# Two moves in a written-out order: a roping pulled ahead of the first heads' sums, and a turn of keys ahead of a rounding of weights

## The chip, the cores and the metric

The kernel runs on one core of a Trainium2 chip. The metric is device time in microseconds (us) from start to end of one execution, lower is better. The engines named here are TensorE (PE in the profile, with its weight loads as PEld), VectorE (DVE), ScalarE (ACT), GpSimd (POOL) and SyncE (SP), whose queue issues the loads of weights.

## The reference, cut to what matters

Two small networks of two layers each run one after the other on 256 tokens of width 1024. The second mixer of the first network is block attention ("moba"). With 256 tokens there is one block of 256 keys, so it is causal attention with 16 heads of 64:

```python
qkv = (h @ w_qkv).reshape(Bsz, S, 3, N_HEADS, HEAD_DIM)
...
q = rope(q, pos) * (HEAD_DIM ** -0.5)
k = rope(k, pos)
...
s_own = jnp.einsum('bhqd,bhjd->bhqj', qc, ko).astype(jnp.float32)
s_own = jnp.where(kpos[None, :] <= qpos[:, None], s_own, NEG_INF)
p = jax.nn.softmax(jnp.concatenate([s_sel, s_own], axis=-1), axis=-1).astype(v.dtype)
...
return o @ w_o
```

`rope` multiplies the two halves of each head by cosines and sines: `[x1*cos - x2*sin, x2*cos + x1*sin]`. All else (short convolution, feed-forward layers, state space mixer, two further attentions) is left as it is by the change.

## The kernel before, in words

Every weight matrix comes in chunks of 128 x 2048 numbers. A chunk is loaded by SyncE into one of 4 buffers, rounded by ScalarE to a high part (line 1273, one of 5 buffers), and the rest is made on VectorE as a low part (line 1623, one of 4 buffers). TensorE multiplies high by high, high by low and low by high (line 1022): a projection step `tK.T` takes the 128 rows of the contraction with number K for the 128 tokens of tile T and is three matmuls of 512 columns here. SyncE's load number i waits until both parts of chunk i-4 are made.

The order of all work is one list of steps, read by all engines. Each engine goes through the whole list and issues its own share of each step, in order, with waits on semaphores. For the block attention this list is written out by hand as a text, `MOBA`. Its stages are `q0 k0 v0 q1 k1 v1 moba_out`: queries, keys and values of heads 0 to 7, the same of heads 8 to 15, and the output projection. The words that matter here:

- `ropeH.Q.T`: VectorE ropes the queries (Q=1) or keys (Q=0) of half H, tile T, from an accumulator in PSUM to SBUF: four multiplies (lines 1815 to 1818), a wait for them, and two sums (lines 1820 and 1821). The four ropings of a half go through one counter, in the order of the list.
- `crossH.Q.I`: TensorE turns two pairs of heads of the roped queries or keys (line 1107, four transposes), which needs both tiles of that roping and the one bank that the turns and the turned probabilities share; ScalarE copies the result out (line 1363 for queries, 1368 for keys of the second half). The next turn needs that copy.
- `+h`: ScalarE rounds the next chunk (1273), after the last use of the buffer. `+l`: VectorE makes the next low part (1623).
- `sN`: TensorE's scores of heads N and N+1 (1063), VectorE's maxima (1787) and ScalarE's exponentials (1343, 1345). `nN`: VectorE normalises head N (1795 to 1798).
- `dN wN rN` (heads 0 to 7): VectorE turns squares of the probabilities (1806), GpSimd's queue writes them to DRAM (2153) and reads them back in the other order (2160). `uN` (heads 8 to 15): TensorE turns the probabilities itself (1073), ScalarE copies them.
- `p3`, `p7`: TensorE's sums of values for heads 0 to 3 and 4 to 7 (1097), ScalarE's rounding of them (1356), VectorE's low part (1737). `p7` needs the probabilities of heads 4 to 7 read back.

`t_bank_free` says what a stage's first step needs of the bank that it writes. For `v1` it is the roping of the second queries of the same tile:

```python
"v1": lambda: (s_rope, ROPE_AT["rope", 1, 1, t]),
```

In `k1` and `v1`, the numbered chunks used below are: 59 and 60 are the two chunks of `v1` itself; 61 to 64 are those of `moba_out`; chunk 61's low part is the first `+l` of `v1` and 62's the second; chunk 64's rounding is the `+h` beside `t4.0`.

Of the kernel before, what the change touches and what calls it, by code (L numbers as in the profile page):

```python
# [160 lines left out]
t7.1  # L161
@q1 t0.0 n1 d1 w0 t0.1 t1.0 +h w1 t1.1 t2.0 r0 +l +l vcopy0 t2.1 s2 n2 r1 d2 t3.0 t3.1 w2 t4.0 n3 d3 t4.1 t5.0 s4 w3 r2
t5.1 t6.0 t6.1 n4 d4 r3 +h +l +h t7.0 t7.1
@k1 t0.0 s6 w4 n5 d5 rope1.1.0 t0.1 t1.0 t1.1 w5 t2.0 t2.1 t3.0 t3.1 t4.0 n6 d6 t4.1 t5.0 p3 r4 r5 w6 t5.1 +h +l r6 t6.0 t6.1
t7.0 t7.1
@v1 t0.0 rope1.1.1 t0.1 cross1.1.0 t1.0 n7 d7 rope1.0.0 +h w7 t1.1 rope1.0.1 +l t2.0 r7 t2.1 cross1.1.1 t3.0 +l t3.1 +h t4.0 cross1.0.0
t4.1 s8 +l t5.0 cross1.0.1 n8 t5.1 p7 s10 t6.0 u8 vcopy1 t6.1 t7.0 n9 t7.1 n10
@moba_out s12 u9 t0.0 t0.1 n11 n12 +h t1.0 +l u10 t1.1 n13 u11 t2.0 p11 u12 s14 n14 n15 +l u13 t2.1 t3.0 +h p13 u14
t3.1 u15 e4 p15 e5 e6 e7 +l +h end
# [2155 lines left out]
```

## Time and profile before

| | us |
|---|---|
| median of 3 runs | 1201.04 (1200.89 to 1201.39) |
| the profiled execution, its own time | 1200.93 |
| span of the profiled execution | 1199.6 |
| TensorE busy (matmuls) | 1189.0 |
| VectorE, ScalarE, GpSimd busy | 885.4, 657.8, 63.1 |

The profile is of one execution. Busy time is the time in which an engine had an instruction in work; matmuls overlap one another, so a start of one often lies a little before the end of the last. Times in the trace count from the start of the span. A row of the timeline gives start, duration, engine, line, operation, output and input, the number of instructions merged, and in brackets the idle time before and what ended it.

### The profile page before, as it was taken

How to read it: one execution, taken by the hardware profiler on the slowest of the kernel's cores; microseconds unless marked ns; L12 is line 12 of the kernel's file. 1: busy time of each engine (PE TensorE's matmuls, PEld its weight loads, DVE VectorE, ACT ScalarE, POOL GpSimd, SP SyncE). 2: the span in 40 equal slices, each digit the busy share in tenths (PEclk: the TensorE clock that was granted, in tenths of full speed). 3: DMA queues.
4: the chain of work that ended last, by engine and by line, in shares of the span. 5: the costliest groups of instructions: out<-in, count | busy, mean ns of one | idle time of the engine just before them, and what ended most of it. 6: DMA issues, size and time to landing. Idle time of an engine off the chain costs nothing.

```text
span 1199.6 us, 16810 instructions
## 1 busy us (share of the span) xinstructions
PE 1189.0 (99%) x6733; PEld 1024.5 (85%) x6733; DVE 885.4 (74%) x1238; ACT 657.8 (55%) x863; POOL 63.1 (5%) x91
## 2 busy tenths in 40 slices
PE   9999999999999999999999999999999999999997
PEld 8888888888777888888898888888889978888886
DVE  6977989846886798883688877776467667777744
ACT  6545666634556666663588645444337775544430
POOL 0000000000120000000005200000012001000000
PEclk9999999999999999999999999999999999999999
DMA  9755455564654555556434556555526542755530
GB/s 355 253 207 193 170 182 191 186 224 160 228 181 157 189 178 176 207 191 216 163 109 142 188 207 237 193 193 194 178 91 229 176 141 106 252 204 176 195 122 35
DMA packets 33821, 221.09 MB, mean 184 GB/s; under 512 B 4032, under 2 KB 4432, under 8 KB 9168
## 3 DMA queue, kind: packets, MB, share of 16 engines
q1 hardware_dynamic: 30848, 210.52, 50.1%
q0 software_dynamic: 2752, 9.44, 2.3%
q8 instruction: 53, 0.87, 0.3%
q14 instruction: 24, 0.20, 0.0%
q10 hardware_dynamic: 144, 0.07, 0.0%
HBM read 217.37 MB, written 2.62 MB: 183 GB/s over the span
## 4 chain that ended last, share of the span: by engine, by line
PE 98%; DVE 1%; DMA 1%; ACT 0%; issue 0%; SPq 0%; ACTq 0%
PE ps L1022 42%; PE ps L944 24%; PE ps L950 15%; PE ps L952 4%; PE ps L966 2%; PE ps L963 2%; PE ps L962 2%; PE ps L1063 1%; PE ps L1097 1%; PE ps L1036 1%; PE ps L1073 1%; DMA t<-in_wts 1%; PE ps L1162 0%; PE ps L1146 0%; PE ps L977 0%; PE ps L1044 0%
## 5 line engine op out<-in xcount | busy, mean ns | idle before, releaser
L1022 PE MATMUL ps<-t,t 128*128 128x512 f32 (+4 forms) x2346 | 536.0, 385 | 1.4 <-DVE t L1821 1.4
L1623 DVE TENSOR_TENSOR t<-t,t 128x2048 fp32r<-128x2048 f32 (+3 forms) x200 | 448.9, 2257 | 101.2 <-PE ps L1022 87.7
L1022 PEld LDWEIGHTS ps<-t,t 128*128 128x128 f32 x2346 | 424.8, 188 | 84.4 <-issue 2.8
L1273 ACT CAST t<-t 128x2048 fp32r<-128x2048 f32 (+3 forms) x200 | 374.5, 1882 | 203.6 <-PE ps L1022 104.0
L944 PE MATMUL ps<-t,t 128*128 128x512 f32 x1274 | 305.8, 390 | 0.0
L944 PEld LDWEIGHTS ps<-t,t 128*128 128x128 f32 x1274 | 238.9, 188 | 51.2
L950 PEld LDWEIGHTS ps<-t,t 128*128 128x128 f32 x1456 | 187.2, 191 | 7.4
L950 PE MATMUL ps<-t,t 128*128 128x256 f32 x1456 | 189.5, 283 | 0.0
L1772 DVE TENSOR_REDUCE t<-ps 128x512 f32<-128x1024 f32 x40 | 49.0, 1225 | 44.3 <-PE ps L952 44.3
L1725 DVE SCALAR_TENSOR_TENSOR t<-t,t,t 128x254 f32<-128x254 f32 (+1 forms) x176 | 73.2, 479 | 10.2 <-ACT t L1298 10.2
L1338 ACT CAST t<-t 128x512 fp32r<-128x512 f32 x44 | 27.3, 619 | 91.2 <-DVE t L1756 91.2
L2124 POOL TENSOR_TENSOR t<-t,t 128x1 f32<-128x1 f32 x22 | 15.0, 681 | 868.0 <-DVE t L1678 455.4
L1737 DVE TENSOR_TENSOR t<-t,t 128x512 fp32r<-128x512 f32 x48 | 33.2, 693 | 35.0 <-ACT t L1338 32.2
L952 PE MATMUL ps<-t,t 128*128 128x512 f32 x182 | 58.0, 397 | 0.0
L962 PE MATMUL ps<-t,t 128*128 128x256 f32 x192 | 49.0, 288 | 0.0
L963 PE MATMUL ps<-t,t 128*128 128x256 f32 x192 | 48.0, 283 | 0.0
L1334 ACT ACTIVATE t<-t 128x512 f32<-128x512 f32 x42 | 26.4, 628 | 29.2 <-DVE t L1725 29.2
L1298 ACT ACTIVATE t<-t,t 128x256 f32<-128x256 f32 x88 | 39.7, 500 | 1.6 <-DVE t L2066 1.6
L963 PEld LDWEIGHTS ps<-t,t 128*128 128x128 f32 x192 | 36.7, 191 | 0.5 <-issue 0.2
L962 PEld LDWEIGHTS ps<-t,t 128*128 128x128 f32 x192 | 36.7, 191 | 0.5 <-issue 0.2
L1557 ACT CAST t<-ps 128x512 fp32r<-128x512 f32 x28 | 15.6, 588 | 34.9 <-PE ps L1036 34.8
L966 PE MATMUL ps<-t,t 128*128 128x256 f32 x192 | 30.9, 283 | 0.0
(228 smaller groups left out, 846.0 us busy)
## 6 DMA issues: line engine op xcount, KB each, us to landing
t<-in_wts SPq DMA_DIRECT2D x192, 1024.0 KB, 5.0
t<-in_rows POOLq DMA_DIRECT2D x12, 512.0 KB, 4.3
t<-in_wts SPq DMA_DIRECT2D x4, 528.0 KB, 3.8
spilled_probs<-t POOLq DMA_DIRECT2D x8, 192.0 KB, 4.1
t<-spilled_probs POOLq DMA_DIRECT2D x8, 192.0 KB, 4.1
t<-in_wts SPq DMA_DIRECT2D x2, 768.0 KB, 4.6
t<-in_wts SPq DMA_DIRECT2D x2, 592.0 KB, 3.8
t<-in_x_in SPq DMA_DIRECT2D x2, 512.0 KB, 4.4
```

Of the source, the lines that this page charges most:

```text
L944: mm(ps[:, bank + m, :], H[:, kt, cols[m]], XT[:, kt, :, :].rearrange("p c s -> p (c s)"), start=kt == order[0], stop=False)
L950: mm(ps[:, bank + m, 0:S], L[:, kt, cols[m]], XTh[:, kt, :], start=False, stop=False)
L952: ins = mm(ps[:, bank + m, :], H[:, last, cols[m]], XT[:, last, :, :].rearrange("p c s -> p (c s)"), start=False, stop=True)
L962: mm(o, H[:, kt, c], XTh[:, kt, :], start=kt == 0, stop=False)
L963: mm(o, L[:, kt, c], XTh[:, kt, :], start=False, stop=False)
L966: ins = mm(o, H[:, kt, c], XTl[:, kt, :], start=False, stop=kt == 7)
L1022: ins = mm(ps[:, bank, at:at + c1 - c0], a, w[:, k, c0:c1], start=first and part == 0, stop=kt == KTS[stage] - 1 and part == 2)
L1273: copy(wh[:, k, 0:w], wraw[:, r, 0:w]).then_inc(s_hi, 1)
L1298: activation(dst[:, sl], src[:, sl], ACT.Copy, scale=vcol(name, col + blk)).then_inc(done, 1)
L1623: tt(wl[:, k, 0:w], wraw[:, r, 0:w], wh[:, h, 0:w].bitcast(F32), ALU.subtract).then_inc(s_lo, 1)
L1725: ins = stt(out=o, in0=src[:, blk * S:(blk + 1) * S - n], scalar=vcol(name, col + blk + (taps - 1 - n) * stride), in1=o, op0=ALU.mult, op1 ...
L1772: nc.vector.reduce_sum(dst.rearrange("p (a s) -> p a s", a=2), halves, AX_X).then_inc(s_wide, 1)
```

## The change

Two words move in the list. `rope1.1.1`, VectorE's roping of the second queries of tile 1, moves from `v1` (behind `t0.0`) to `k1` (behind `d6`), so that on VectorE it stands ahead of the low part of the sums of heads 0 to 3 (`p3`) and of chunk 60's low part (`+l`). `cross1.0.0`, the first turn of the second keys, moves from behind `+h t4.0` to ahead of it, so that on TensorE it stands ahead of `t4.0` and on ScalarE ahead of the rounding of chunk 64.

```diff
-@k1 t0.0 s6 w4 n5 d5 rope1.1.0 t0.1 t1.0 t1.1 w5 t2.0 t2.1 t3.0 t3.1 t4.0 n6 d6 t4.1 t5.0 p3 r4 r5 w6 t5.1 +h +l r6 t6.0 t6.1
+@k1 t0.0 s6 w4 n5 d5 rope1.1.0 t0.1 t1.0 t1.1 w5 t2.0 t2.1 t3.0 t3.1 t4.0 n6 d6 rope1.1.1 t4.1 t5.0 p3 r4 r5 w6 t5.1 +h +l r6 t6.0 t6.1
 t7.0 t7.1
-@v1 t0.0 rope1.1.1 t0.1 cross1.1.0 t1.0 n7 d7 rope1.0.0 +h w7 t1.1 rope1.0.1 +l t2.0 r7 t2.1 cross1.1.1 t3.0 +l t3.1 +h t4.0 cross1.0.0
+@v1 t0.0 t0.1 cross1.1.0 t1.0 n7 d7 rope1.0.0 +h w7 t1.1 rope1.0.1 +l t2.0 r7 t2.1 cross1.1.1 t3.0 +l t3.1 cross1.0.0 +h t4.0
 t4.1 s8 +l t5.0 cross1.0.1 n8 t5.1 p7 s10 t6.0 u8 vcopy1 t6.1 t7.0 n9 t7.1 n10
```

No instruction is added or removed. The order of the four ropings and of the four turns among themselves stays.

## Rows read from the trace of the kernel before

**Rows 1.** Page, busy time of the engines
```profile
PE 1189.0 (99%) x6733; PEld 1024.5 (85%) x6733; DVE 885.4 (74%) x1238; ACT 657.8 (55%) x863; POOL 63.1 (5%) x91
```

**Rows 2.** Waits of TensorE, whole span: waiter, releaser, total, times, longest
```profile
PE ps L1022 <- DVE t L1821: 1.4, 1, 1.4
PE ps L1063 <- ACT t L1368: 0.8, 1, 0.8
```

**Rows 3.** Chain that ended last, 341 to 366 us: start, us, what
```profile
359.59 0.69 PE ps L1022 x3
...
361.74 0.86 PE ps L1063 x8
```

**Rows 4.** Timeline of TensorE, k1 and v1
```profile
342.89 4.42 PE L1022 MATMUL ps<-t,t 128*128 128x512 f32 x18
348.69 0.96 PE L1022 MATMUL ps<-t,t 128*128 128x512 f32 x3 [1.39 <-DVE t L1821]
...
355.57 0.95 PE L1022 MATMUL ps<-t,t 128*128 128x512 f32 x3
357.33 0.93 PE L1063 MATMUL ps<-t,t 64*128 64x128 f32 x8 [0.81 <-ACT t L1368]
...
360.21 1.53 PE L1097 MATMUL ps<-t,t 128*64 128x128 f32 x24
```

**Rows 5.** Timeline of VectorE, k1 and v1
```profile
343.62 0.69 DVE L1737 TENSOR_TENSOR t<-ps,t 128x512 fp32r<-128x512 f32 x1 [2.73 <-ACT t L1356]
...
346.43 0.42 DVE L1815 TENSOR_TENSOR t<-ps,t 128x256 f32<-128x256 f32 x1
...
348.22 0.42 DVE L1821 TENSOR_TENSOR t<-t,t 128x256 f32<-128x256 f32 x1
348.55 0.16 DVE L1795 RECIPROCAL t<-t 128x2 f32<-128x2 f32 x1
...
353.91 0.42 DVE L1821 TENSOR_TENSOR t<-t,t 128x256 f32<-128x256 f32 x1
354.25 4.49 DVE L1623 TENSOR_TENSOR t<-t,t 128x2048 fp32r<-128x2048 f32 x2
...
362.36 0.35 DVE L1798 TENSOR_SCALAR t<-t,t 128x256 f32<-128x256 f32 x1
...
366.79 0.29 DVE L1787 CUSTOM_DVE_ANT_0 t<-ps,t 128x128 f32<-128x128 f32 x1 [1.06 <-PE ps L1063]
```

**Rows 6.** Timeline of ScalarE, v1
```profile
353.34 0.59 ACT L1363 COPY t<-ps 128x512 f32<-128x512 f32 x1 [0.81 <-PE ps L1107]
354.79 1.91 ACT L1273 CAST t<-t 128x2048 fp32r<-128x2048 f32 x1 [0.86 <-PE ps L1022]
356.60 0.58 ACT L1368 COPY t<-ps 128x512 f32<-128x512 f32 x1
```

**Rows 7.** Timeline of TensorE's weight loads, v1
```profile
354.99 0.59 PEld L1107 LDWEIGHTS ps<-t,t 128*128 128x128 f32 x4
...
363.10 0.48 PEld L1073 LDWEIGHTS ps<-t,t 128*128 128x128 f32 x3
```

**Rows 8.** Timeline of GpSimd, read of head 6, write and read of head 7
```profile
348.23 0.75 POOL L2160 DMA_DIRECT2D t<-spilled_probs  x1 [2.63 <-DMA spilled_probs<-t]
350.28 0.56 POOL L2153 DMA_DIRECT2D spilled_probs<-t  x1 [1.30 <-DVE t L1806]
354.09 0.75 POOL L2160 DMA_DIRECT2D t<-spilled_probs  x1 [3.25 <-DMA spilled_probs<-t]
```

**Rows 9.** Timeline of SyncE's queue, load of chunk 65
```profile
356.60 0.33 SPq L2240 DMA_DIRECT2D t<-in_wts  x1
```

**Rows 10.** DMA issues: head 7's read; head 3's write; all reads (last number us to landing)
```profile
t<-spilled_probs POOLq DMA_DIRECT2D x1, 192.0 KB, 2.9
...
spilled_probs<-t POOLq DMA_DIRECT2D x1, 192.0 KB, 6.8
...
DMA to landing us min/median/max: 2.9/4.1/7.1
```

## The prediction

> **What bounds the kernel now.** I read the page first: TensorE is busy 1189.0 of a span of 1199.6 us [rows 1]. So only two things can move the time: one of the few places where TensorE stands still, or a new one. The next view is the list of what TensorE waited for over the whole span. It is very short, and two of its entries are the places that the diff touches [rows 2]: 1.4 us before a projection matmul, ended by the last sum of a roping (line 1821), and 0.8 us before scores (line 1063), ended by ScalarE's copy of a turn of keys (line 1368). Third I read the timelines of the engines from 340 to 367 us, to name the steps. The 18 matmuls from 342.89 are t5.1 to t7.1 of k1 and t0.0 of v1; what starts at 348.69 is t0.1 of v1; what starts at 357.33 is s8 [rows 4].
>
> **Why TensorE stands still at t0.1.** It writes the bank of the second queries of tile 1, so it needs rope1.1.1. VectorE has that roping behind the low part of p3 and chunk 60's low part. It stands idle for 2.73 us until 343.62, waiting for ScalarE's rounding of p3, then does both, and starts rope1.1.1 at 346.43. The roping ends at 348.22 + 0.42 = 348.64, and t0.1 starts 0.05 us later [rows 4, 5].
>
> **Why it stands still at s8.** The scores need the copy of cross1.0.0. ScalarE finished the copy of cross1.1.1 at 353.93, stood idle 0.86 us until t3.1 freed a buffer, rounded chunk 64 from 354.79, and only then copied, from 356.60 to 357.18 [rows 6]. The scores start 0.15 us later [rows 4].
>
> **First edit: what the roping costs and frees.** In its place it holds VectorE from 346.43 to the start of the next instruction at 348.55, which is 2.12 us; to its own end it is 2.21 us [rows 5]. Its new place is the idle stretch before 343.62, which began at 343.62 - 2.73 = 340.89, with d6. Its queries have been in PSUM since the end of q1, and rope1.1.0 is done. So it would run from 340.9 to 343.1, and the low part of p3 can start at 343.62 as before, with 0.5 us to spare. That idle stretch is the cover, and the move costs nothing. Were the cover gone, it would cost at most what it costs now, and t0.1 would wait as before. t0.1 then needs nothing late, and follows t0.0.
>
> The gain at this place is more than the 1.39 us of idle, since a stream that starts anew must fill again. The last matmul before the gap ends at 342.89 + 4.42 = 347.31, the three of t0.1 at 348.69 + 0.96 = 349.65 [rows 4]; in a running stream three take 0.69 us end to end [rows 3]. 349.65 - 347.31 - 0.69 = **1.65 us**. The bounds are 1.39 (idle alone) and 1.65; I take 1.65, as both ends of it are rows.
>
> VectorE's queue behind the old place (n7, d7, rope1.0.0, rope1.0.1, the low parts of chunks 61 and 62, the maxima of s8) starts 2.12 us earlier. I checked the one step in it that could meet TensorE: rope1.0.0 needs the end of k1, which is one projection step before 347.31, so 346.6; it would start after n7 and d7 at about 347.8. So the whole queue keeps its 2.12 us.
>
> **Second edit.** On TensorE cross1.0.0 comes three matmuls earlier, on ScalarE one rounding earlier. TensorE is 1.65 us early there. In the trace the weights of cross1.0.0 load from 354.99 [rows 7]; three matmuls and 1.65 us earlier that is 354.99 - 0.69 - 1.65 = 352.65. It needs two things. The roping rope1.0.1 ended at 353.91 + 0.42 = 354.33 [rows 5], and 2.12 earlier is 352.21. The copy of cross1.1.1 ended at 353.93 [rows 6], and 1.65 earlier is 352.28. Both are there with 0.37 us left, against 0.05 us that a release took above. The copy of cross1.0.0 then runs on ScalarE from about 353.5 to 354.1. TensorE reaches s8 at 355.57 + 0.95 = 356.52 less 1.65, so 354.87: the copy is 0.8 us early. Gain at s8: the scores end at 357.33 + 0.93 = 358.26; from the end of t4.1 at 356.52 they need 0.86 in a running stream [rows 3, 4]: 358.26 - 356.52 - 0.86 = **0.88 us**. The bounds are 0.81 (idle) and 0.88. Without the first edit the turn's weights would want to load at 354.30 with the roping ending at 354.33, so the second edit doesn't hang on the first.
>
> The rounding of chunk 64 moves behind the copy, to about 354.1, still 0.7 us earlier than the 354.79 of now. VectorE wants it only behind v1's last matmuls. It costs nothing.
>
> **What is late next.** From s8 on TensorE is 1.65 + 0.88 = 2.53 us early and VectorE only 2.12, so VectorE's lead shrinks by 0.41 us. The maxima of s8 and n8 feed the turn of head 8's probabilities (u8), whose weights load from 363.10, while n8 ends at 362.36 + 0.35 = 362.71 [rows 5, 7]. With 0.05 for the release 0.34 us are free and 0.41 are wanted: a new stall of **0.07 us**. Its bounds are 0 and 0.41. Past s12 VectorE has waited 1.06 us for TensorE [rows 5], so there it has room again, and the two lock together.
>
> The other late one is p7, which needs head 7's probabilities back from DRAM. GpSimd's queue has read 6, write 7, read 7. The write went out at 350.28, 1.30 us after the read of head 6, because it waited for d7. With d7 2.12 early it follows that read at once, at 348.23 + 0.75 = 348.98. Write and wait for it took 354.09 - 350.28 = 3.81 us, so the read goes out at about 352.8 and lands 2.9 us later at 355.7 [rows 8, 10]. p7 began at 360.21 [rows 4] and would begin at 357.68. There are 2.0 us left, where 3.2 were.
>
> But traffic moves too. SyncE's load of chunk 65 hangs on the low part of chunk 61, which ends 2.12 us earlier, so it goes out at 356.60 - 2.12 = 354.5 [rows 9], 1.7 us behind the read, where it was 2.5 behind. Reads of the same size took between 2.9 and 7.1 us in this trace [rows 10]. At 7.1 the read would land at 359.9 and p7 wait 2.2 us. I take 0, since a load starts to move bytes only after the read in front of it has moved most of its own. Here a rule speaks against the change: the Trainium skill, DMA: Bandwidth & Descriptors, section Queues, rings and completion order, says that each DMA engine goes round between the queues that have work, a packet at a time, so a small read gets no right of way over a 1 MB load. The spread of 2.9 to 7.1 us fits it; by that rule a read caught by the load would take the long figure, and the sum below would fall from 2.46 to 0.3 us.
>
> **The sum.** 1.65 + 0.88 - 0.07 = 2.46 us. Everything behind the block attention hangs on TensorE and moves with it. Span 1199.6 becomes 1197.1, the profiled execution's 1200.93 becomes 1198.5; it lies 0.11 under the median of 1201.04, which becomes **1198.6**. What this measurement can tell from no change is about 0.2%, 2.4 us, so a time of 1198.64. The forecast lies right on that line.
>
> **Rivals.**
>
> *VectorE becomes the pace-setter* (0.10). If the 0.34 us at u8 is not really free, all that counts is VectorE's own 2.12 us. Speaks for it: from 343.62 to 365.7 it has no idle time. Against: n8's end and the load of u8 are rows. Time 1201.04 - 2.12 = 1198.9.
>
> *p7 waits for part of the round trip, or cross1.0.0 for its copy* (0.14). A read between its 2.9 and 7.1 us, or a write that the nearer load holds up, eats 0.5 to 2.2 us; the 0.37 us at cross1.0.0 could also be missed. Time 1199.1 to 1200.8, middle 1200.0. Against: in the run before this read was the fastest of the eight.
>
> *The change does nothing* (0.07). If t0.1 waits at the same time for something else that ends then, or p3's low part slips, the wait stays. Against: the release is 0.05 us after the roping's end, and the same chunk served t0.0. Time 1201.0.
>
> *Slower* (0.05). The write of head 7 now goes out at 348.98, into the load of chunk 64, and its read near the load of chunk 65. The longest write read here took 6.8 and the longest read 7.1 us [rows 10]: 348.98 + 6.8 + 7.1 = 362.9 against p7's 360.21 of before, 2.7 us later, 1203.7. It decides as soon as the round trip is over 360.21 - 348.98 = 11.2 us; it was 6.7. It would need both extremes at once.
>
> *More than forecast* (0.04): the stall at u8 is not there and a restart costs more than the ends show, 2.6 to 2.9 us, 1198.3.
>
> The forecast itself has 0.60, with a range of 1198.2 to 1199.1.
>
> **How the numbers follow.** Half of the forecast's 0.60 lies under the 1198.64 line, somewhat more as the value is under it by a hair: 0.38; with the last rival that is 0.42 for faster. The other part of the forecast, the pace-setter, the partial waits and no effect make 0.53. Slower has 0.05. The range goes from 1198.1, under the last rival's time, up to 1200.5, which takes in most of the partial waits and leaves out no effect, slower and a rest: about 0.15.
>
> **What the profile after would show.** TensorE's list of waits without both entries, or with one of about 0.1 us at line 1073; a roping that starts at 340.9 right behind a turn of squares on VectorE; the low part of p3 at 343.6 as before; line 1107's third turn of v1 right behind six matmuls, and ScalarE's copy at line 1368 ahead of the rounding; s8 near 354.9 and p7 near 357.7. Wrong would be a wait of line 1097 for a DMA, a wait of line 1107 for line 1363 or 1821, or a wait of line 1022 still at v1's start.

## The result, and the profile after

The median of the changed kernel is 1203.95 us (1200.94 to 1206.28, 20 executions), that of the kernel before 1201.19 us (1200.77 to 1204.86, 20). The ratio is 1.0018, with a 95% interval of 1.001 to 1.0025. It is slower by 0.18% (0.23% by the two medians), beyond the interval but about the 0.2% that I had called no change, and far from the 1198.6 forecast. The profiled execution took 1204.28 us with a span of 1203.0, 3.4 more than before.

What TensorE waited for over the whole span, the first four entries (waiter, releaser, total, times, longest):

```profile
PE ps L1097 <- DMA t<-spilled_probs: 4.4, 1, 4.4
PE ps L1243 <- DVE t L1997: 1.2, 1, 1.2
PE ps L977 <- DMA t<-in_wts: 0.5, 1, 0.5
PE ps L1206 <- ACT t L1503: 0.2, 1, 0.2
```

Both entries of [rows 2] are gone. A new one of 4.4 us stands in their place: the sums of heads 4 to 7 (p7) wait for the read of probabilities from DRAM. The timeline of TensorE, k1 and v1, against [rows 4]:

```profile
343.10 5.11 PE L1022 MATMUL ps<-t,t 128*128 128x512 f32 x21
348.04 0.60 PE L1107 MATMUL ps<-t,t 128*128 128x128 f32 x4
...
354.99 0.93 PE L1063 MATMUL ps<-t,t 64*128 64x128 f32 x8
...
356.99 0.95 PE L1022 MATMUL ps<-t,t 128*128 128x512 f32 x3
362.33 2.82 PE L1097 MATMUL ps<-t,t 128*64 128x128 f32 x24 [4.39 <-DMA t<-spilled_probs]
```

The 18 matmuls of before run on into t0.1 as 21 without a gap, and s8 starts without one. This execution is 0.21 us later than the other at the start of this stretch (343.10 against 342.89). t5.1, the last projection step ahead of p7, ends at 357.94; before it ended at 360.28 (from the chain: 359.59 + 0.69 [rows 3]). So TensorE was 2.34 + 0.21 = 2.55 us ahead. Then it stood still to 362.33, and p7 took 2.82 us instead of 1.53.

VectorE, ScalarE and their order, against [rows 5] and [rows 6]:

```profile
341.03 0.39 DVE L1815 TENSOR_TENSOR t<-ps,t 128x256 f32<-128x256 f32 x1
...
342.79 0.42 DVE L1821 TENSOR_TENSOR t<-t,t 128x256 f32<-128x256 f32 x1
343.83 0.69 DVE L1737 TENSOR_TENSOR t<-ps,t 128x512 fp32r<-128x512 f32 x1 [0.63 <-ACT t L1356]
...
352.33 4.49 DVE L1623 TENSOR_TENSOR t<-t,t 128x2048 fp32r<-128x2048 f32 x2
```

```profile
353.70 0.59 ACT L1368 COPY t<-ps 128x512 f32<-128x512 f32 x1 [1.24 <-PE ps L1107]
354.22 1.91 ACT L1273 CAST t<-t 128x2048 fp32r<-128x2048 f32 x1
```

The roping fills VectorE's idle stretch and leaves 0.63 us of it; the copy of keys runs ahead of the rounding. All that is as forecast. The GpSimd queue and one row of SyncE's queue, against [rows 8] and [rows 9]:

```profile
348.93 0.75 POOL L2160 DMA_DIRECT2D t<-spilled_probs  x1 [3.12 <-DMA spilled_probs<-t]
349.67 0.56 POOL L2153 DMA_DIRECT2D spilled_probs<-t  x1
355.55 0.75 POOL L2160 DMA_DIRECT2D t<-spilled_probs  x1 [5.32 <-DMA spilled_probs<-t]
```

```profile
354.69 0.33 SPq L2240 DMA_DIRECT2D t<-in_wts  x1
```

The write of head 7 goes out right behind the read of head 6, as forecast (at 349.67 and not at 348.98, since that read itself went out later), but landed 5.6 us later, where it had taken 3.5. So its read went out at 355.55, later than before, and now 0.9 us behind the load of chunk 65, which had gone out 2.5 us behind it. It took 6.7 us instead of 2.9. DMA issues of that write and that read (last number: us to landing), against [rows 10]:

```profile
spilled_probs<-t POOLq DMA_DIRECT2D x1, 192.0 KB, 5.6
...
t<-spilled_probs POOLq DMA_DIRECT2D x1, 192.0 KB, 6.7
```

Four stretches of the same trace (stretch, its length, busy times with instructions of PE, PEld, DVE, ACT and POOL, then PEclk, the granted TensorE clock as a share of 2.4 GHz, and last the busy share and the GB/s of the DMA engines):

```profile
360.00:361.00 1.00, 0.00 (x0) 0.00 (x0) 0.76 (x4) 0.00 (x0) 0.00 (x0) 1.00 0.86 347
361.00:362.00 1.00, 0.00 (x0) 0.00 (x0) 0.00 (x0) 0.00 (x0) 0.00 (x0) 0.80 1.03 401
362.00:363.00 1.00, 0.67 (x7) 0.70 (x9) 0.00 (x0) 0.00 (x0) 0.00 (x0) 0.50 0.90 336
...
365.00:366.00 1.00, 1.00 (x11) 0.59 (x9) 0.20 (x1) 0.59 (x1) 0.00 (x0) 1.00 0.16 66
```

While TensorE stood idle its clock fell to 1.2 GHz, and p7 ran wholly at that level. It is back in the stretch from 365.00, while p7 ends at 365.15. The Trainium skill, TensorE: Matmul & The Clock Gate, section Part 1: The HAM clock gate, says that an idle array falls to half its clock; the trace agrees. The loss adds up: the scores behind p7 end at 366.00, where they ended at 362.60 before, 3.40 us later, and the spans differ by the same 3.4.

### The profile page after: what moved, and what is told of

The parts are those of the page before. It is cut to its first block, busy times and chain, and to the rows that moved or that the text cites. A ratio compares the mean times of both kernels' runs of the same rounds, so it can differ in the third digit from the quotient of the medians.

```text
span 1203.0 us, 16810 instructions
## 1 busy us (share of the span) xinstructions
PE 1190.3 (99%) x6733; PEld 1026.0 (85%) x6733; DVE 885.6 (74%) x1238; ACT 658.9 (55%) x863; POOL 63.5 (5%) x91
## 4 chain that ended last, share of the span: by engine, by line
PE 97%; DMA 2%; DVE 0%; POOL 0%; issue 0%; ACT 0%; SPq 0%; POOLq 0%
PE ps L1022 42%; PE ps L944 24%; PE ps L950 14%; PE ps L952 4%; PE ps L966 2%; PE ps L963 2%; PE ps L962 2%; PE ps L1063 1%; PE ps L1097 1%; PE ps L1036 1%; PE ps L1073 1%; DMA spilled_probs<-t 1%; DMA t<-spilled_probs 1%; DMA t<-in_wts 1%; PE ps L1162 0%; PE ps L1146 0%
```

## The experiments

My theory after the result: head 7's round trip through DRAM is late, since its write runs into the load of chunk 64 and its read into the load of chunk 65, both of which the earlier roping brought together. The rivals: the moved turn does harm by itself; the round trip is long whatever the loads do; the earlier order of GpSimd's queue (write beside the read of head 6) is the cause. Edits are against the kernel before for e1, e2, e7 and e10, and against the changed kernel for the others, unless said.

**e1_rope_only.** The first edit alone.

```diff
-... n6 d6 t4.1 t5.0 p3 ...      @v1 t0.0 rope1.1.1 t0.1 ...
+... n6 d6 rope1.1.1 t4.1 t5.0 p3 ...      @v1 t0.0 t0.1 ...
```

> Only the roping is moved, the turn of keys stays where it was. Theory (read-back): TensorE gains 1.65 us at t0.1, the 0.8 us wait of the scores s8 stays, and the sums p7 then wait for head 7's read, whose write now goes out right behind the read of head 6, into the load of chunk 64, and which itself meets the load of chunk 65. Since the landing of the read sets the start of p7, the time is that of the full change, about 1203.9 (1202 to 1205), with a wait of 3 to 4 us at line 1097. Rival (the turn is what hurts, since it delays ScalarE's rounding of chunk 64): this kernel is faster than before, about 1199.5, with no wait at line 1097.

Measured: 1201.21 us (1200.56 to 1205.94), ratio 1.0007 (0.9998 to 1.0015). The profile shows the wait of p7, but of 1.0 us only, with a write of 5.3 and a read of 5.0 us, and a wait of 1.3 us at s8. The time is under the range that I expected. Of the 1.65 us of gain p7's wait took 1.0 and the longer wait at s8 (1.3 instead of 0.8) another 0.5, so p7 waits for the round trip as the theory has it, but for far less than I expected. The longer wait at s8 has a cause that I had not seen. ScalarE's rounding of chunk 64 waited for the load itself:

```profile
353.89 1.91 ACT L1273 CAST t<-t 128x2048 fp32r<-128x2048 f32 x1 [1.41 <-DMA t<-in_wts]
355.69 0.58 ACT L1368 COPY t<-ps 128x512 f32<-128x512 f32 x1
```

The load of chunk 64 took 7.0 us instead of 5.6. That the moved write did this isn't shown: in e2, with the write at its old place, the load took 7.2. With the turn ahead of the rounding, as in the full change, TensorE doesn't wait for this load.

**e2_turn_only.** The second edit alone.

```diff
-... t3.0 +l t3.1 +h t4.0 cross1.0.0
+... t3.0 +l t3.1 cross1.0.0 +h t4.0
```

> Only the turn of keys is moved. Theory (read-back): VectorE's queue and so head 7's write, its read and the load of chunk 65 keep their times; TensorE gains the 0.88 us at s8 and p7 still starts after the landing: about 1200.3, no wait at line 1097. Rival (the turn hurts): slower than before, 1202 or more.

Measured: 1200.98 us (1200.49 to 1201.1), ratio 0.9997 (0.9989 to 1.0006). The rival falls: the turn does no harm, and the read took 2.8 us. But I missed the gain, too. The wait for the copy is gone and a new one stands three steps on:

```profile
362.41 0.35 DVE L1798 TENSOR_SCALAR t<-t,t 128x256 f32<-128x256 f32 x1
...
362.91 0.52 PE L1073 MATMUL ps<-t,t 128*128 128x128 f32 x3 [0.27 <-DVE t L1798]
```

u8 starts at 362.91 instead of 363.33, 0.42 us earlier and not 0.88 (0.07 of it was there before, at t0.1): VectorE, not moved here, sets the pace from n8 on. The median moved by 0.11 us only; the rest of the 0.35 isn't accounted for. The prediction had the 0.34 us of room there; I didn't carry it into this expectation.

**e3_loads_later.** The full change with later low parts of chunks 61 to 63.

```diff
-... rope1.0.1 +l t2.0 r7 t2.1 cross1.1.1 t3.0 +l t3.1 cross1.0.0 +h t4.0 t4.1 s8 +l t5.0 cross1.0.1 n8 t5.1 p7 ...
+... rope1.0.1 t2.0 r7 t2.1 cross1.1.1 t3.0 t3.1 cross1.0.0 +h t4.0 t4.1 s8 t5.0 +l cross1.0.1 n8 t5.1 +l p7 ...
-... n11 n12 +h t1.0 +l u10
+... n11 n12 +h +l t1.0 +l u10
```

> The full change, and beside it VectorE's low parts of chunks 61 and 62 behind the maxima of s8 and that of chunk 63 behind n12, so that the loads of chunks 65 to 67 go out some 4 us and more later. The load of chunk 64, and with it the neighbourhood of head 7's write, stays. Theory (the read is held up by the load of chunk 65): the read lands in about 3 us instead of 6.7, p7 waits about 1 us or less and the clock of TensorE stays up: about 1199.5 (1198.6 to 1200.5). Rival (the round trip is long by itself, or by the load of chunk 64 alone): p7 waits 3 us or more, time as with the change, 1203 to 1204.

Measured: 1199.74 us (1199.6 to 1200.98), ratio 0.9987 (0.9978 to 0.9996), 4.2 us under the full change. The last write and the last read of its GpSimd queue, and the landing of that read:

```profile
349.90 0.56 POOL L2153 DMA_DIRECT2D spilled_probs<-t  x1
357.24 0.75 POOL L2160 DMA_DIRECT2D t<-spilled_probs  x1 [6.78 <-DMA spilled_probs<-t]
```

```profile
t<-spilled_probs POOLq DMA_DIRECT2D x1, 192.0 KB, 2.9
```

The load of chunk 65 went out at 359.66 and the read took 2.9 us. The write took 7.1 us beside the load of chunk 64, so p7 still waited 2.1 us in this execution, which is the slowest of its eleven. That is half of the theory: the read, met by no load, is short again.

**e4_write_early.** The full change, with head 7 normalised, turned and written ahead of the moved roping, and read right behind head 6.

```diff
-@k1 ... n6 d6 rope1.1.1 t4.1 t5.0 p3 r4 r5 w6 t5.1 +h +l r6 t6.0 t6.1
+@k1 ... n6 d6 w6 n7 d7 w7 rope1.1.1 t4.1 t5.0 p3 r4 r5 t5.1 +h +l r6 r7 t6.0 t6.1
-@v1 t0.0 t0.1 cross1.1.0 t1.0 n7 d7 rope1.0.0 +h w7 t1.1 rope1.0.1 +l t2.0 r7 t2.1 ...
+@v1 t0.0 t0.1 cross1.1.0 t1.0 rope1.0.0 +h t1.1 rope1.0.1 +l t2.0 t2.1 ...
```

> The full change, and beside it n7 and d7 right behind d6 on VectorE, ahead of the moved roping, the writes of heads 6 and 7 ahead of the reads of heads 4 and 5 and the read of head 7 right behind that of head 6 on the GpSimd queue. VectorE gets some 0.8 us more work ahead of the low part of p3 than its idle stretch holds, all of it work that it then has no more behind. Theory (read-back): the read lands by 353, p7 waits for nothing, and the 2.5 us that TensorE gains at t0.1 and s8 are all seen: 1198.6 (1198.2 to 1199.2). Rival (something else in the change costs time, as the turn or the clock): 1200 or more.

Measured: 1198.55 us (1198.38 to 1198.84), ratio 0.9979 (0.997 to 0.9987): faster than both kernels. Its start of p7 and its writes and reads:

```profile
356.92 0.95 PE L1022 MATMUL ps<-t,t 128*128 128x512 f32 x3
357.80 1.53 PE L1097 MATMUL ps<-t,t 128*64 128x128 f32 x24
```

```profile
341.32 0.54 POOL L2153 DMA_DIRECT2D spilled_probs<-t  x1 [2.88 <-DVE t L1806]
342.64 0.54 POOL L2153 DMA_DIRECT2D spilled_probs<-t  x1 [0.78 <-DVE t L1806]
343.68 2.99 POOL L2160 DMA_DIRECT2D t<-spilled_probs  x4 [0.49 <-PE ps L1097]
```

Both writes go out while no load is in flight and take 2.1 us each. Neither entry of [rows 2] nor one at line 1097 is in its list of waits. The gain of 2.5 us that the prediction worked out is all seen once the round trip is out of the way.

**e5_sums_later.** The full change, with p7 behind s10 and t6.0.

```diff
-... t5.1 p7 s10 t6.0 u8 vcopy1 t6.1
+... t5.1 s10 t6.0 p7 u8 vcopy1 t6.1
```

> The full change, and beside it the sums p7 two places later in the list (behind s10 and t6.0 instead of ahead of them), about 1.8 us of TensorE's work. Writes, reads and loads stay. Theory (read-back): the read lands as late as with the change, but the work put ahead of p7 fills 1.8 us of its wait, and where the wait that is left is short the clock does not fall: 1200.3 to 1202.2, about 1201.5. Rival (it is not the landing that sets p7 but the length of the list): no change against the full change, 1203.9.

Measured: median 1199.5 us (1199.2 to 1205.01), ratio 0.9994 (0.9985 to 1.0004). The rival falls, and the gain is more than I expected: in the profiled execution, the fastest of its eleven, write and read took 5.1 and 5.3 us, the wait was 0.4 us, and the clock stayed up. Some executions still reach 1205.

**e6_write_first.** The full change, with head 7's write ahead of head 6's read on the GpSimd queue.

```diff
-... t5.1 +h +l r6 t6.0 t6.1      ... rope1.0.0 +h w7 t1.1 ...
+... t5.1 +h +l t6.0 t6.1      ... rope1.0.0 +h w7 r6 t1.1 ...
```

> The full change, and beside it the write of head 7 ahead of the read of head 6 on the GpSimd queue, so that it goes out at about 348.2 instead of 349.7 and the read of head 6 goes behind it. The load of chunk 64 is in flight as before. Theory A (the write is slow because the read of head 6 runs beside it): the write lands in 4 us or less, by 352.3, and the read of head 7 goes out ahead of the load of chunk 65 at 354.7 and lands by 356: about 1198.8. Theory B (the write is slow because of the load of chunk 64): the write still takes 5 to 6 us, lands at 353.5 to 354, and the read then meets the load of chunk 65: 1200 to 1203.

Measured: 1202.62 us (1198.37 to 1206.17), ratio 1.0012 (1.0 to 1.0024). The write went out at 348.10, ahead of the read, and took 6.5 us beside the load of chunk 64 (out at 346.54). The time that theory A gave did not come. The run doesn't take the read of head 6 away, though: it went out at 348.75 and ran beside the write all the same, so e8 has to decide between A and B. Two of the twelve executions took 1198.37 and 1198.57 us, which is the full gain. The wait at p7 in the profiled one, and the clock:

```profile
360.12 2.83 PE L1097 MATMUL ps<-t,t 128*64 128x128 f32 x24 [2.45 <-DMA t<-spilled_probs]
```

```profile
361.00:362.00 1.00, 1.00 (x13) 1.00 (x12) 0.00 (x0) 0.00 (x0) 0.00 (x0) 0.50 1.03 418
```

**e7_before_early_write.** The kernel before with the early write of e4 and nothing else.

> The kernel before, with only n7 and d7 early on VectorE and the writes of heads 6 and 7 and the read of head 7 early on the GpSimd queue; the roping and the turn stay where they were before. Theory: the wait for the roping at t0.1 is left as it is, as the low part of p3 and of chunk 60 start at the same time; VectorE's queue behind the roping is 1.35 us earlier; the wait at s8 stays: 1200.5 to 1201.1. The read is then never the last to come, so the executions should lie within about 0.5 us of each other, where those of the kernel before reach up to 1204.9. If the outliers stay, they are of another cause than the read.

Measured: 1201.14 us (1200.84 to 1201.68), ratio 1.0 (0.9991 to 1.0009). That is a hair above the range that I expected: the early write is worth nothing by itself. Its executions lie within 0.84 us, but those of the kernel before beside it reached only 1202.5, so whether the read makes the rare executions of 1204 us of the kernel before stays open.

**e8_load64_later.** As e3, with the low part of chunk 60 behind rope1.0.0.

```diff
-... w6 t5.1 +h +l r6 t6.0 t6.1      ... n7 d7 rope1.0.0 +h w7 t1.1 ...
+... w6 t5.1 +h r6 t6.0 t6.1      ... n7 d7 rope1.0.0 +l +h w7 t1.1 ...
```

> As the kernel with the later loads (loads of chunks 65 to 67 later), and beside it VectorE's low part of chunk 60 behind rope1.0.0, so that the load of chunk 64 goes out at about 351.3 instead of 346.8, behind the write of head 7. Theory B (the write is slow because of the load of chunk 64): the write takes 3 to 3.5 us and lands by 353.2; the read of head 7 then goes out at 353.5 and meets the load of chunk 64 instead, taking 3 to 6 us. Theory A (the read of head 6 beside it is enough): the write takes 5 us or more. The time is a mix, as rope1.0.1 now ends at 353.4 and cross1.0.0 waits for it about 0.7 us: 1199.3 to 1202.

Measured: 1200.26 us (1200.08 to 1200.85), ratio 0.9992 (0.9984 to 1.0001). The write and the read of head 7 on the GpSimd queue, and the landing of the write:

```profile
349.38 0.56 POOL L2153 DMA_DIRECT2D spilled_probs<-t  x1
352.53 0.75 POOL L2160 DMA_DIRECT2D t<-spilled_probs  x1 [2.59 <-DMA spilled_probs<-t]
```

```profile
spilled_probs<-t POOLq DMA_DIRECT2D x1, 192.0 KB, 2.9
```

The read of head 6 went out beside it as before (at 348.65), but the load of chunk 64 only 1.7 us behind it (at 351.07), and the write took 2.9 us. Theory A falls here. That is the other half, from one profiled execution: it is a load of chunk 64 already in flight that holds the write up. p7 waited for nothing. The rest of the gain went to waits on VectorE's and ScalarE's later work (0.3 at a turn, 0.5 at s12, 0.7 at u9).

**e9_early_write_rope and e10_early_write_turn.** e4 with one of the two edits each (e4 with `+h t4.0 cross1.0.0` as before; e7 with `cross1.0.0 +h t4.0`).

> The kernel with the early write of head 7, with the roping moved and the turn of keys left where it was before. With the read-back off the path, the roping's own term should stand by itself: 1.65 us under the median of before, 1199.4, and the wait at s8 of about 0.8 us is back in the list of TensorE's waits. Rival (the terms are not additive, s8's wait follows the load of chunk 64): up to 1200.

> The kernel with the early write of head 7, with the turn of keys moved and the roping left where it was before. VectorE's queue behind the roping is 1.35 us earlier here than in the kernel with the turn alone, so the stall at u8 that took most of the 0.88 us there should be gone: 0.88 us under the median of before, 1200.2, and no wait at line 1073. Rival (the turn is worth only 0.1 to 0.3 us by itself): 1200.8 to 1201.0.

Measured: e9 1199.8 us (1199.53 to 1202.25), ratio 0.9985 (0.9976 to 0.9994); e10 1200.27 us (1199.87 to 1200.97), ratio 0.999 (0.9981 to 0.9999). e10 is 0.76 us under the 1201.03 of the kernel before beside it, near its 0.88, and has no wait at line 1073, which fits the room at u8 as what took the gain away in e2. e9 gains 1.23 instead of 1.65, as its rival had it. Its profiled execution shows how: s8 waits 1.7 us, since ScalarE's rounding in front of the copy waits 1.8 us for the load of chunk 64. But that execution is the slowest of its eleven (1202.25 us), so the size of the wait in the others isn't known. With both edits the copy is ahead of that rounding, and the sum is 2.5.

The landings side by side, each from one profiled execution (out, and us to landing):

```
              load 64        head 7's write   load 65   head 7's read   p7 waited
before        346.59  5.6    350.28  3.5      356.60    354.09  2.9     0
after         346.80  7.4    349.67  5.6      354.69    355.55  6.7     4.4
rope only     346.84  7.0    349.61  5.3      354.72    355.22  5.0     1.0
turn only     346.52  7.2    350.34  4.5      356.66    355.08  2.8     0
loads later   347.04  9.1    349.90  7.1      359.66    357.24  2.9     2.1
sums later    346.52  6.8    349.16  5.1      354.41    354.58  5.3     0.4
write first   346.54  7.5    348.10  6.5      354.43    354.85  5.1     2.4
load 64 later 351.07  5.1    349.38  2.9      359.65    352.53  4.2     0
write early   347.32  6.4    342.64  2.1      353.89    345.92  3.1     0
before, early 346.74  5.9    342.65  2.1      355.65    345.92  4.9     0
early, rope   347.31  6.8    342.63  2.1      353.88    345.89  3.3     0
early, turn   346.56  7.3    342.47  2.1      355.48    345.74  5.6     0
```

The last four rows are e4, e7, e9 and e10. Start and duration added give the landings, and these say more than the durations. With the read of head 6 ahead of it and the load of chunk 64 in flight, the write of head 7 landed 1.6 us behind that load before, and 0.8 to 1.1 us behind it in the five others (after, rope only, turn only, loads later, sums later). When the write itself went out, between 349.2 and 350.3, made next to no difference: with the rope only it went out 0.7 us earlier than with the turn only, and landed 0.1 us later. And the load's own duration, 5.6 to 9.1 us, doesn't follow the moved write: it was 7.2 with the write at its old place (turn only) and 7.3 with the write long landed and a read beside it (early, turn). Why it varies isn't shown. Of the reads with no load in flight ahead of them, those that a load followed by 0.8 us took 4.9 and 5.6 us, those that one followed by 1.4 us or more 2.8 to 3.3.

## Why the prediction was wrong

**Right, by its steps.** The cause of both waits, the cover of the roping (0.5 us to spare forecast, 0.63 seen), the 1.65 + 0.88 = 2.53 us on TensorE's side (2.55 seen at t5.1), the turn with its two needs met, and the copy at 353.70 against "about 353.5". The stall of 0.07 us at u8 never came to the test in the full change, as p7's wait hid it; e2 shows that the room of 0.34 us is real.

**The step that failed** is the one on p7: "Write and wait for it took 354.09 - 350.28 = 3.81 us, so the read goes out at about 352.8", and then "I take 0". I moved the write 1.3 us nearer to the load of chunk 64 and kept the duration of its old place. Behind that load it took 5.1 to 7.1 us in the five profiled executions where it went out at 348.1 to 349.9 (five rows of the table), and 2.9 ahead of it (e8). Its landing followed that of the load: the write went out 0.6 us earlier than before and landed 1.5 us later, at 355.26, as the load itself landed at 354.20 instead of 352.21. So the earlier roping brought the read nothing, while it did bring the load of chunk 65 forward by 1.9 us. The second half follows from the first. "I take 0" held for the order that it assumed: in e2, with the load 1.6 us behind the read, the read took 2.8 us. But by the forecast the read was 1.7 us ahead of the load of chunk 65; by the late write it came 0.9 us behind it, and took 6.7 instead of 2.9 us (2.9 again in e3). The rule of the Trainium skill that I had set beside it (DMA: Bandwidth & Descriptors, section Queues, rings and completion order: engines take turns between queues by packets) was against me here: a read caught by the load got no right of way. The traces agree in the durations, 5.0 to 6.7 us for the four reads that went out 0.2 to 0.9 us behind the load; none of them was read down to the turns of the queues.

**The rival that came true** is the slower one, with a chance of 0.05. Its mechanism and place were right and its chance was far too small, for two reasons. I said that it needed both extremes at once (6.8 + 7.1), but its own threshold of 11.2 us was already passed by 12.5 (349.67 to 362.20). And I took the two transfers as independent, where a late write is what puts the read behind the load. Its price lacked a term as well: the clock at 1.2 GHz made p7 last 2.82 us instead of the 1.53 that it took at full clock behind the wait of e3, 1.3 us more. So it is partly luck that its 1203.7 lies next to the measured 1203.95: it had p7 at 362.9, later than the 362.33 seen, and nothing for the clock.

**What stays open.** The full change takes 2.7 us more in the median than the roping alone, where I expected the same. In the profiled executions p7 starts 2.0 us later and the clock costs 1.3. Why its read should be the longer one in most executions, when both order the same transfers at nearly the same times, isn't shown. The traces give two hints. In the full change the read went out 0.9 us behind the load of chunk 65 and 1.3 ahead of that of chunk 66, and landed 2.5 us after the first; with the rope only it was 0.5 and 1.7, and the read landed 0.5 us after the first. So it may have met both loads. And the same landing costs more in the full change: its TensorE is at p7 by 357.94, and the landing at 360.19 of the rope only would leave it idle for some 2.4 us (an estimate from these two), as long as the wait in e6 behind which the clock was down.

## What to carry to other kernels

When a step moves, don't move its DMA's duration with it: the same 192 KB write took 2.1 us with the queues empty and up to 7.1 beside a 1 MB load, and there it landed about 1 us behind the load, whether it had gone out at 349.2 or at 350.3. So look at what is in flight at the new time, and at which load the freed engine releases earlier. A round trip that was hidden with 3 us to spare is the next bound once TensorE gets 2.5 us ahead; put its start ahead of the gain (here ahead of the moved roping, into the same idle stretch), and both come out, 1198.55 us. And a wait behind which TensorE's clock is down costs more than its own length, here 1.3 us more.

## What the runs showed of the hardware that I had not expected

After its wait at p7, TensorE ran at 1.2 GHz behind 4.39 us and behind 2.45 us of idle (e6), but not behind 2.12 us (e3, p7 in 1.53 us). In the profiled execution of e9 it fell about a microsecond after a wait of only 1.69 us at s8 had ended (granted clock 0.92 from 357 to 358, 0.50 from 358 to 361), and in e1 it stayed up with waits of 1.34 and 0.96 us. So the length of the wait alone doesn't say whether the clock falls.
